# An expert layer in light positions: the down product one block later, the high half of the gated tile rounded by ScalarE

## The chip, the core and the metric

One core of a Trainium2 chip runs the whole program. The metric is the device time of one execution in microseconds; lower is better. TensorE multiplies, ScalarE and VectorE prepare its operands, and weights come from HBM through 16 DMA engines that SyncE's queue feeds.

## What is computed

The reference is an encoder trunk of two layers. Layer 0 ends in a dense SwiGLU, layer 1 in eight experts, of which each of the 256 tokens uses two:

```python
def swiglu(h, w1, w3, w2):
    return (jax.nn.silu(h @ w1) * (h @ w3)) @ w2

def moe_swiglu(h, w_router, w1, w3, w2):
    ...
    for e in range(N_EXPERTS):
        out = out + combine[..., e:e + 1] * swiglu(h, w1[e], w3[e], w2[e])
```

with model width 1024 and expert width 3584. The change touches the expert layer alone, which runs from about 700 us to the end.

## The kernel before

Every product is computed from operands that are split in two: `hi`, the value rounded to TensorE's format, and `lo`, the rest. A weight tile of 1 MB (128 x 2048 f32, an "item") is loaded into one of 7 `raw` buffers, ScalarE rounds it to `whi` (L1726), VectorE subtracts to get `wlo` (L2359), and TensorE uses both. `whi` and `wlo` have 3 slots (SPLIT), so the rounding of item n waits until TensorE has finished item n - 3. The load of item n + 7 is issued when `wlo` of item n is there (L1369). One list, `e_items`, fixes the order of items for all engines; each engine's program is written out by hand, and `e_room(phase, kind, n)` says how many items an engine may prepare before it has to do the named step.

Experts are visited in eight positions, `ROLES = "HLHLHLHH"`. A heavy position has room for 128 rows and uses hi and lo of the rows as separate operands. A light one has 64 rows and packs their hi and lo halves side by side into one 128-wide operand, so it needs two products where a heavy one needs three. Positions 1, 3 and 5 are light ("first", "second" and "third" light position below).

The expert width is cut into NM = 7 blocks (0 to 6). For each block there are six items: two halves of w1, two of w3, two of w2. In a position, TensorE does for block b = 1 to 6: `up` w1 b, `hidden_T` b - 1 (L1206: folds the packed halves and transposes them into the bank eT), `up` w3 b, `down` b - 1 (L1230). Then, in the tail: `up` w1 0 of the next position, `hidden_T` 6, `up` w3 0 of the next position, `down` 6. In blocks 1 to 6 and the tail one position takes 42 items; they are numbered 0 to 41 below, in the order in which they are used.

In a light position the gated tile of a block goes: ScalarE `silu_folded` (L1742), then on VectorE a multiplication into `gated_t` (L2385), the rounding of `gated_t` into the high half of `gated_m` (L2388), and the subtraction for its low half (L2390), which counts `g_lo` up; `down` waits for `g_lo`. All engines are strictly in order, so an instruction that waits holds back everything behind it on its engine.

Items before (`e_items`), in the lines that the change replaces:

```python
def mid_items(p):
    return [i for b in range(1, NM) for i in halves(p, ("w1", b), ("w3", b), ("w2", b - 1))]
...
    e_items += mid_items(p) + (head_items(p + 1) if p < LAST else []) + halves(p, ("w2", NM - 1))
```

Of the kernel before, what the change touches and what calls it, by code (L numbers as in the profile page):

```python
# [33 lines left out]
F32 = mybir.dt.float32  # L34
# [9 lines left out]
LIGHT = 64  # L44
# [202 lines left out]
def build(nc, x, mem, positions, g_mix, w_in, g_q, g_kv, w_uq, w_uk, w_uv, g_sg, w_s, b_s, g_mem,  # L247
# [31 lines left out]
    with ExitStack() as ctx:  # L279
# [285 lines left out]

        def halves(p, *blocks):
            return [(p, kind, b, half) for kind, b in blocks for half in range(2)]
# [4 lines left out]
        def mid_items(p):  # L572
            return [i for b in range(1, NM) for i in halves(p, ("w1", b), ("w3", b), ("w2", b - 1))]

        e_items = head_items(0)
        for p in range(NE):
            e_items += mid_items(p) + (head_items(p + 1) if p < LAST else []) + halves(p, ("w2", NM - 1))
# [120 lines left out]
        def _(pe):  # L698
# [467 lines left out]
            def is_light(phase):  # L1166
                return phase != "over" and light[phase]

# [84 lines left out]
            def blocks(phase, j=0):  # L1253

                for b_ in range(1, NM):
                    up(phase, "w1", b_, j)
                    if b_ == 1 and phase != "over" and phase and light[phase - 1]:
                        fold_result(phase - 1)
                    hidden_T(phase, b_ - 1, j)
                    if phase != "over" and phase < LAST and b_ == NM - 1:  # L1260

                        pe.wait_ge(slots_moved, 32 * phase + 16)
                        rows_T(phase + 1)
                    up(phase, "w3", b_, j)
                    if phase == LAST and b_ == NM - 1:
                        down(phase, b_ - 1, j, (0,))
                        hidden_T(phase, b_, j)
                        down(phase, b_ - 1, j, (1,))
                    else:
                        down(phase, b_ - 1, j)  # L1270
                    if phase == LAST and b_ == 2:
                        select_T(phase, j)
# [27 lines left out]
            for p in range(NE):  # L1300
                blocks(p)
                if p < LAST:
                    up(p + 1, "w1", 0, 0, lambda half: read(pe, (p + 1, "rows", half)))
                    hidden_T(p, NM - 1)
                    up(p + 1, "w3", 0)
                    down(p, NM - 1)
# [170 lines left out]
        def _(act):  # L1477
# [251 lines left out]
            def is_light(phase):  # L1729
                return phase != "over" and light[phase]  # L1730

# [11 lines left out]

            def copy_gate(p, b_):

                b = full(act, (p, "e3", b_))
                free(nc.scalar.activation(g32_m, b[:, :], ACT.Copy), (p, "e3", b_))

            def hidden_hi(phase, b_, j=0):

                b = full(act, (phase, "eT", b_), j)
                nc.scalar.activation(gated_m[0][:, b_ % 2, :], b[:, :], ACT.Copy).then_inc(g_hi, 1)
# [25 lines left out]
            def blocks(phase, j=0):  # L1778

                for b_ in range(1, NM):  # L1780
                    e_hi(e_room(phase, "e1", b_), j)
                    if is_light(phase):
                        e_hi(e_room(phase, "eT", b_ - 1), j)
                        silu_folded(phase, b_ - 1)
# [38 lines left out]
            for p in range(NE - 1):  # L1823
# [6 lines left out]
                if light[p]:  # L1830
                    e_hi(e_room(p, "eT", NM - 1))
                    silu_folded(p, NM - 1)
                e_silu(p + 1, 0)
                if not light[p]:
                    e_hi(e_room(p, "eT", NM - 1))
                    hidden_hi(p, NM - 1)
# [36 lines left out]
        def _(dve):  # L1873
# [489 lines left out]
            def is_light(phase):  # L2363
                return phase != "over" and light[phase]

# [7 lines left out]

            def hidden_lo(phase, b_, j=0):
# [5 lines left out]
                count = NM * (NE if phase == "over" else phase) + b_ + 1 + NM * j  # L2380
                if is_light(phase):
                    dve.wait_ge(silu_t_ready, light_block(phase, b_))
                    if light_block(phase, b_) > 1:
                        dve.wait_ge(g_lo, light_block(phase, b_) - 1)
                    free(V.tensor_tensor(gated_t, silu_t, b[:, BM * LIGHT:2 * BM * LIGHT], ALU.mult), (phase, "eT", b_))  # L2385
                    read(dve, (phase, "eT", b_))
                    part, by_chunk = by_slot(gated_m[0][:, b_ % 2, :]), gated_t.rearrange("p (c s) -> p c s", c=BM)
                    V.tensor_copy(part[:, :, 0:LIGHT], by_chunk).then_inc(g_hi, 1)  # L2388
                    dve.wait_ge(g_hi, count)
                    V.tensor_tensor(part[:, :, LIGHT:2 * LIGHT], by_chunk, part[:, :, 0:LIGHT].bitcast(F32),  # L2390
                                    ALU.subtract).then_inc(g_lo, 1)
                    return
                dve.wait_ge(g_hi, count)
# [36 lines left out]
            def blocks(phase, j=0):  # L2430

                for b_ in range(1, NM):
                    e_lo(e_room(phase, "e1", b_), j)
                    hidden_lo(phase, b_ - 1, j)
                    e_lo(e_room(phase, "e3", b_), j)
                    if phase != "over" and phase < LAST and b_ == NM - 1:
                        rows_lo(phase + 1)
                    hidden(phase, b_, j)
# [26 lines left out]
            for p in range(NE - 1):  # L2465
                blocks(p)
                e_lo(e_room(p + 1, "e1", 0))
                hidden_lo(p, NM - 1)
                e_lo(e_room(p + 1, "e3", 0))
                hidden(p + 1, 0)  # L2470
            dve.wait_ge(flag_ready, 1)
# [79 lines left out]
```

## Time and profile before

| | |
|---|---|
| median of 3 runs | 1626.28 us (1625.83 to 1626.38) |
| profiled execution | 1627.45 us |
| its span | 1625.6 us |
| TensorE busy, of the span | 97% |
| VectorE busy | 79% |
| ScalarE busy | 65% |
| mean granted TensorE clock | 0.994 |
| load, median from issue to landing (expert weights) | 8.0 us |

The span goes from the first to the last instruction; the 1.85 us between it and the profiled time lie around it. Busy shares are means over stages with different limits. A clock of 1.00 is 2.4 GHz, 0.50 is 1.2 GHz. In a timeline a line has start, length, engine, source line, operation, out<-in and count, and in brackets how long the engine sat idle before it and what ended that. A length includes the drain of the pipeline, so the next instruction of an engine can start before it is over; the pace of a row of instructions is read from starts. A line of a windows view has the stretch, its length, the busy time and count of TensorE (matmuls, then weight loads), VectorE, ScalarE and GpSimd, then TensorE's granted clock, the DMA share and GB/s.

### The profile page before, as it was taken

The numbers are of one execution on the slowest core, as the hardware profiler recorded it, in microseconds if no ns is written. First come the engines' busy times: TensorE is split into PE (matmuls) and PEld (weight loads), VectorE is DVE, ScalarE is ACT, GpSimd is POOL, SyncE is SP. The second block draws the span as 40 slices with busy tenths as digits, with TensorE's granted clock in tenths as the row PEclk, the third lists the DMA queues.
The fourth block names the chain that finished last, engine by engine and source line by source line (L and its number), as shares of the span: only waits on it lengthen the run. The fifth ranks groups of instructions, "written<-read, shape, count | busy, mean of one in ns | idle before, by whom it ended". The sixth has DMA issues, their size and how long they took to land.

```text
span 1625.6 us, 21020 instructions
## 1 busy us (share of the span) xinstructions
PE 1577.1 (97%) x8224; PEld 1336.8 (82%) x8224; DVE 1279.1 (79%) x1204; ACT 1057.5 (65%) x988; POOL 30.5 (2%) x69
## 2 busy tenths in 40 slices
PE   9999999999999999999999999999999999999997
PEld 8988888999989888778877778777788777788885
DVE  6676666555576756688899988899888999888997
ACT  6555445333355554557788877788777888777774
POOL 1000000000000000020000000000000000000100
PEclk9999999999999999999999999999999999999998
DMA  7654478977355535669999999999999999999992
GB/s 234 216 193 143 143 241 277 311 246 228 126 169 173 180 118 182 251 233 423 395 386 421 421 417 386 375 420 420 422 387 393 387 421 421 416 386 367 407 396 116
DMA packets 143112, 497.48 MB, mean 306 GB/s; under 512 B 8534, under 2 KB 64400, under 8 KB 100000
## 3 DMA queue, kind: packets, MB, share of 16 engines
q1 hardware_dynamic: 137008, 479.23, 77.8%
q0 software_dynamic: 2624, 8.45, 1.5%
q10 hardware_dynamic: 3376, 8.39, 1.3%
q8 instruction: 68, 1.11, 0.3%
q14 instruction: 36, 0.29, 0.1%
HBM read 476.64 MB, written 19.40 MB: 305 GB/s over the span
## 4 chain that ended last, share of the span: by engine, by line
PE 73%; DVE 18%; ACT 4%; issue 3%; DMA 1%; ACTq 0%; POOL 0%; SPq 0%; DVEq 0%; POOLq 0%
PE bank L730 22%; PE bank L1187 15%; PE bank L1230 13%; DVE wlo L2359 12%; PE bank L901 9%; PE bank L1191 8%; ACT whi L1726 2%; ACT whi L1493 1%; PE bank L720 1%; DVE wlo L1915 1%; PE bank L1015 1%; PE bank L1210 1%; PE bank L1206 1%; DMA hn<-in_mem 1%; ACT pbuf L1628 0%
## 5 line engine op out<-in xcount | busy, mean ns | idle before, releaser
L2359 DVE TENSOR_TENSOR wlo<-raw,whi 128x2048 fp32r<-128x2048 f32 x328 | 739.9, 2287 | 73.0 <-ACT whi L1726 72.4
L1726 ACT ACTIVATE whi<-raw 128x2048 fp32r<-128x2048 f32 x328 | 623.9, 1916 | 160.2 <-PE bank L1191 83.1
L1915 DVE TENSOR_TENSOR wlo<-raw,whi 128x2048 fp32r<-128x2048 f32 (+3 forms) x121 | 259.3, 2148 | 176.3 <-ACT whi L1493 175.9
L1493 ACT ACTIVATE whi<-raw 128x2048 fp32r<-128x2048 f32 (+3 forms) x121 | 217.7, 1801 | 145.8 <-PE bank L730 103.3
L1187 PE MATMUL bank<-whi,yT_hi 128*128 128x512 f32 x896 | 312.2, 396 | 0.0
L1191 PE MATMUL bank<-wlo,yT_hi 128*128 128x512 f32 x896 | 241.3, 391 | 2.9 <-DVE wlo L1915 2.8
L1187 PE MATMUL bank<-whi,yT_lo 128*128 128x512 f32 x560 | 216.7, 390 | 0.0
L1230 PE MATMUL bank<-whi,yT_hi 128*128 128x512 f32 x448 | 180.2, 402 | 25.7 <-DVE yT_hi L2390 16.4
L1191 PEld LDWEIGHTS bank<-wlo,yT_hi 128*128 128x128 f32 x896 | 168.3, 188 | 39.9 <-DVE wlo L1915 3.2
L1187 PEld LDWEIGHTS bank<-whi,yT_hi 128*128 128x128 f32 x896 | 167.0, 188 | 33.1
L1230 PE MATMUL bank<-wlo,yT_hi 128*128 128x512 f32 x448 | 175.9, 393 | 0.0
L1230 PEld LDWEIGHTS bank<-whi,yT_hi 128*128 128x128 f32 x448 | 84.5, 189 | 60.5 <-DVE yT_hi L2390 24.1
L730 PE MATMUL bank<-hT_hi,whi 128*128 128x256 f32 x464 | 131.4, 283 | 0.0
L730 PE MATMUL bank<-hT_hi,wlo 128*128 128x256 f32 x464 | 131.3, 283 | 0.0
L730 PE MATMUL bank<-hT_lo,whi 128*128 128x256 f32 x464 | 131.3, 283 | 0.0
L1187 PEld LDWEIGHTS bank<-whi,yT_lo 128*128 128x128 f32 x560 | 105.4, 188 | 21.3 <-DVE yT_lo L2298 0.2
L1230 PE MATMUL bank<-whi,yT_lo 128*128 128x512 f32 x280 | 109.0, 389 | 0.0
L1230 PEld LDWEIGHTS bank<-wlo,yT_hi 128*128 128x128 f32 x448 | 84.7, 189 | 16.8
L730 PEld LDWEIGHTS bank<-hT_lo,whi 128*128 128x128 f32 x464 | 89.0, 192 | 0.4
L730 PEld LDWEIGHTS bank<-hT_hi,whi 128*128 128x128 f32 x464 | 89.0, 192 | 0.4
L730 PEld LDWEIGHTS bank<-hT_hi,wlo 128*128 128x128 f32 x464 | 89.0, 192 | 0.0
L730 PE MATMUL bank<-whi,mT_hi 128*128 128x512 f32 (+1 forms) x204 | 79.6, 390 | 0.0
(323 smaller groups left out, 2062.8 us busy)
## 6 DMA issues: line engine op xcount, KB each, us to landing
raw<-in_moe_w SPq DMA_DIRECT2D x336, 1024.0 KB, 8.0
raw<-in_w_in SPq DMA_DIRECT2D x36, 1024.0 KB, 5.3
raw<-in_dense_w SPq DMA_DIRECT2D x30, 1024.0 KB, 6.4
raw<-in_w_br SPq DMA_DIRECT2D x12, 1024.0 KB, 5.0
rows_by_slot<-qxT SPq DMA_DIRECT2D x23, 512.0 KB, 7.0
raw<-in_w_out SPq DMA_DIRECT2D x8, 1024.0 KB, 5.0
raw<-in_w_mkv SPq DMA_DIRECT2D x6, 1024.0 KB, 8.2
cqkv<-rows_by_slot ACTq DMA_DIRECT2D x7, 512.0 KB, 8.5
```

The source lines that it names most:

```text
L720: ins = nc.tensor.matmul(bank, lhs(k), rhs(k), start=(k == 0), stop=(k == n - 1))
L730: ins = nc.tensor.matmul(bank, lhs(a, k), rhs(b, k), start=(start and k == chunks[0] and a + b == 0), stop=(stop and k == chunks[-1] and a ...
L901: ins = nc.tensor.matmul(bank, src(a, x0), w[b_][:, w0, :], start=(start and q + i == 0), stop=(stop and last))
L1015: ins = nc.tensor.matmul(b[:, t * SEQ:(t + 1) * SEQ], qT[0:QK, h, tok(t)], kT[0:QK, h, :], start=True, stop=True)
L1187: nc.tensor.matmul(b[:, :], hselT[a][:, half, tok(k)], w[:, k, :], start=(half + k + a == 0), stop=False)
L1191: ins = nc.tensor.matmul(b[:, :], hselT[0][:, half, tok(k)], w[:, k, :], start=False, stop=(half == 1 and k == 3))
L1206: ins = nc.tensor.matmul(b[:, a:a + LIGHT], src[:, tok(c)], fold[:, 0:LIGHT], start=True, stop=True)
L1230: ins = nc.tensor.matmul(banks[4 + n][:, :], gated_m[a][:, b_ % 2, tok(2 * half + c)], w[p][:, c, n * HALF:(n + 1) * HALF], start=(b_ + ha ...
L1493: nc.scalar.activation(whi[:, m % SPLIT, 0:floats(n)], raw[:, pieces[n][1], 0:floats(n)], ACT.Copy).then_inc(hi_ready, 1)
L1726: nc.scalar.activation(whi[:, (E0 + n) % SPLIT, :], raw[:, n % RAW, :], ACT.Copy).then_inc(hi_ready, 1)
L1915: V.tensor_tensor(wlo[:, m % SPLIT, 0:size], raw[:, pieces[n][1], 0:size], whi[:, m % SPLIT, 0:size].bitcast(F32), ALU.subtract).then_inc( ...
L2359: V.tensor_tensor(wlo[:, s, :], raw[:, n % RAW, :], whi[:, s, :].bitcast(F32), ALU.subtract).then_inc(lo_ready, 1)
```

## The change

In light positions (`light[p]`) the down product of a block runs one block later: w2 b - 2 in block b, nothing in block 1, and w2 5 and w2 6 one after the other in the tail. `hidden_lo` of a light block is divided: `gated` (VectorE) writes `gated_t`, `hidden_hi` on ScalarE rounds it into the high half, and `gated_lo` (VectorE) subtracts one block later. In the tail of a light position the three parts for block 6 follow one another. Heavy positions keep their order. `is_light` moves to one place.

```diff
             return w[0, :, b, half, :, :][e, :, :].unsqueeze(1)
 
 
+        def is_light(phase):
+            return phase != "over" and light[phase]
+
         def halves(p, *blocks):
             return [(p, kind, b, half) for kind, b in blocks for half in range(2)]
 
...
             return halves(p, ("w1", 0), ("w3", 0))
 
         def mid_items(p):
-            return [i for b in range(1, NM) for i in halves(p, ("w1", b), ("w3", b), ("w2", b - 1))]
+            lag = 2 if is_light(p) else 1
+            return [i for b in range(1, NM)
+                    for i in halves(p, ("w1", b), ("w3", b), *([("w2", b - lag)] if b >= lag else []))]
+
+        def tail_items(p):
+            return halves(p, *([("w2", NM - 2)] if is_light(p) else []), ("w2", NM - 1))
 
         e_items = head_items(0)
         for p in range(NE):
-            e_items += mid_items(p) + (head_items(p + 1) if p < LAST else []) + halves(p, ("w2", NM - 1))
+            e_items += mid_items(p) + (head_items(p + 1) if p < LAST else []) + tail_items(p)
         N_E = len(e_items)
         PER_E = N_E // NE
         HEAD = len(head_items(0))
...
                         down(phase, b_ - 1, j, (0,))
                         hidden_T(phase, b_, j)
                         down(phase, b_ - 1, j, (1,))
-                    else:
+                    elif not is_light(phase):
                         down(phase, b_ - 1, j)
+                    elif b_ > 1:
+                        down(phase, b_ - 2)
                     if phase == LAST and b_ == 2:
                         select_T(phase, j)
 
...
                     up(p + 1, "w1", 0, 0, lambda half: read(pe, (p + 1, "rows", half)))
                     hidden_T(p, NM - 1)
                     up(p + 1, "w3", 0)
+                    if light[p]:
+                        down(p, NM - 2)
                     down(p, NM - 1)
             combine(LAST)
             marks["over"] = [count, 0]
...
                 b = full(act, (p, "eT", b_))
                 nc.scalar.activation(silu_t, b[:, 0:BM * LIGHT], ACT.Silu).then_inc(silu_t_ready, 1)
 
+            def hidden_hi(phase, b_, j=0):
+
+                if is_light(phase):
+                    read(act, (phase, "eT", b_))
+                    nc.scalar.activation(by_slot(gated_m[0][:, b_ % 2, :])[:, :, 0:LIGHT],
+                                         gated_t.rearrange("p (c s) -> p c s", c=BM), ACT.Copy).then_inc(g_hi, 1)
+                    return
+                b = full(act, (phase, "eT", b_), j)
+                nc.scalar.activation(gated_m[0][:, b_ % 2, :], b[:, :], ACT.Copy).then_inc(g_hi, 1)
+
             def copy_gate(p, b_):
 
                 b = full(act, (p, "e3", b_))
                 free(nc.scalar.activation(g32_m, b[:, :], ACT.Copy), (p, "e3", b_))
-
-            def hidden_hi(phase, b_, j=0):
-
-                b = full(act, (phase, "eT", b_), j)
-                nc.scalar.activation(gated_m[0][:, b_ % 2, :], b[:, :], ACT.Copy).then_inc(g_hi, 1)
 
             def rows_hi_part(phase, j=0):
 
...
                 for b_ in range(1, NM):
                     e_hi(e_room(phase, "e1", b_), j)
                     if is_light(phase):
-                        e_hi(e_room(phase, "eT", b_ - 1), j)
+                        if b_ > 1:
+                            hidden_hi(phase, b_ - 2)
+                        e_hi(e_room(phase, "eT", b_ - 1))
                         silu_folded(phase, b_ - 1)
                     e_silu(phase, b_, j)
                     if b_ == 1 and phase != "over" and phase and light[phase - 1]:
...
                 rows_hi_part(p + 1)
                 e_hi(e_room(p + 1, "e1", 0))
                 if light[p]:
+                    hidden_hi(p, NM - 2)
                     e_hi(e_room(p, "eT", NM - 1))
                     silu_folded(p, NM - 1)
                 e_silu(p + 1, 0)
-                if not light[p]:
-                    e_hi(e_room(p, "eT", NM - 1))
-                    hidden_hi(p, NM - 1)
+                e_hi(e_room(p + 1, "e3", 0) if light[p] else e_room(p, "eT", NM - 1))
+                hidden_hi(p, NM - 1)
                 if light[p + 1]:
                     e_hi(e_room(p + 1, "e3", 0))
                     copy_gate(p + 1, 0)
...
                 read(dve, (phase, "e1", b_), j)
                 free(V.tensor_tensor(g32_m, silu_m, b[:, :], ALU.mult), (phase, "e3", b_))
 
+            def gated(p, b_):
+
+                b = full(dve, (p, "eT", b_))
+                dve.wait_ge(silu_t_ready, light_block(p, b_))
+                if light_block(p, b_) > 1:
+                    dve.wait_ge(g_lo, light_block(p, b_) - 1)
+                free(V.tensor_tensor(gated_t, silu_t, b[:, BM * LIGHT:2 * BM * LIGHT], ALU.mult), (p, "eT", b_))
+
+            def gated_lo(p, b_):
+
+                dve.wait_ge(g_hi, NM * p + b_ + 1)
+                part = by_slot(gated_m[0][:, b_ % 2, :])
+                V.tensor_tensor(part[:, :, LIGHT:2 * LIGHT], gated_t.rearrange("p (c s) -> p c s", c=BM),
+                                part[:, :, 0:LIGHT].bitcast(F32), ALU.subtract).then_inc(g_lo, 1)
+
             def hidden_lo(phase, b_, j=0):
 
                 end = N_E + PER_E if phase == "over" else N_E
                 last = phase in (LAST, "over") and b_ == NM - 1
                 e_lo(min(e_room(phase, "eT", b_), end - 1 if last else end), j)
                 b = full(dve, (phase, "eT", b_), j)
-                count = NM * (NE if phase == "over" else phase) + b_ + 1 + NM * j
-                if is_light(phase):
-                    dve.wait_ge(silu_t_ready, light_block(phase, b_))
-                    if light_block(phase, b_) > 1:
-                        dve.wait_ge(g_lo, light_block(phase, b_) - 1)
-                    free(V.tensor_tensor(gated_t, silu_t, b[:, BM * LIGHT:2 * BM * LIGHT], ALU.mult), (phase, "eT", b_))
-                    read(dve, (phase, "eT", b_))
-                    part, by_chunk = by_slot(gated_m[0][:, b_ % 2, :]), gated_t.rearrange("p (c s) -> p c s", c=BM)
-                    V.tensor_copy(part[:, :, 0:LIGHT], by_chunk).then_inc(g_hi, 1)
-                    dve.wait_ge(g_hi, count)
-                    V.tensor_tensor(part[:, :, LIGHT:2 * LIGHT], by_chunk, part[:, :, 0:LIGHT].bitcast(F32),
-                                    ALU.subtract).then_inc(g_lo, 1)
-                    return
-                dve.wait_ge(g_hi, count)
+                dve.wait_ge(g_hi, NM * (NE if phase == "over" else phase) + b_ + 1 + NM * j)
                 part = [v[:, b_ % 2, :] for v in gated_m]
                 free(V.tensor_tensor(part[1], b[:, :], part[0].bitcast(F32), ALU.subtract), (phase, "eT", b_))
 
...
 
                 for b_ in range(1, NM):
                     e_lo(e_room(phase, "e1", b_), j)
-                    hidden_lo(phase, b_ - 1, j)
+                    if not is_light(phase):
+                        hidden_lo(phase, b_ - 1, j)
+                    elif b_ > 1:
+                        gated_lo(phase, b_ - 2)
                     e_lo(e_room(phase, "e3", b_), j)
                     if phase != "over" and phase < LAST and b_ == NM - 1:
                         rows_lo(phase + 1)
+                    if is_light(phase):
+                        gated(phase, b_ - 1)
                     hidden(phase, b_, j)
                     if phase == LAST and b_ == 1:
                         last_choice()
...
             for p in range(NE - 1):
                 blocks(p)
                 e_lo(e_room(p + 1, "e1", 0))
-                hidden_lo(p, NM - 1)
+                if light[p]:
+                    gated_lo(p, NM - 2)
+                else:
+                    hidden_lo(p, NM - 1)
                 e_lo(e_room(p + 1, "e3", 0))
+                if light[p]:
+                    gated(p, NM - 1)
                 hidden(p + 1, 0)
+                if light[p]:
+                    gated_lo(p, NM - 1)
             dve.wait_ge(flag_ready, 1)
             overflow = dve.value_load(more[0:1, 0:1], min_val=0, max_val=1)
             blocks(LAST)
```

## Rows read from the trace of the kernel before

**Rows 1.** Profile page: its first line.
```profile
span 1625.6 us, 21020 instructions
```

**Rows 2.** Windows: blocks of the first light position, then a heavy one.
```profile
834.00:918.00 84.00, 77.16 (x379) 61.93 (x378) 82.49 (x55) 72.73 (x56) 0.00 (x0) 1.00 1.01 421
...
942.00:1030.00 88.00, 87.87 (x401) 72.19 (x400) 75.01 (x42) 65.68 (x44) 0.00 (x0) 1.00 1.00 394
```

**Rows 3.** Timeline of VectorE, first light position, blocks 4 to 6.
```profile
884.49 0.41 DVE L2385 TENSOR_TENSOR cT<-cT,bank 128x256 f32<-128x256 f32 x1
884.93 0.29 DVE L2388 CAST yT_hi<-cT 128x256 fp32r<-128x256 f32 x1
885.26 0.43 DVE L2390 TENSOR_TENSOR yT_hi<-cT,yT_hi 128x256 fp32r<-128x256 f32 x1
885.60 13.29 DVE L2359 TENSOR_TENSOR wlo<-raw,whi 128x2048 fp32r<-128x2048 f32 x6
898.81 0.41 DVE L2385 TENSOR_TENSOR cT<-cT,bank 128x256 f32<-128x256 f32 x1
...
914.56 2.29 DVE L2359 TENSOR_TENSOR wlo<-raw,whi 128x2048 fp32r<-128x2048 f32 x1 [0.22 <-ACT whi L1726]
```

**Rows 4.** Timeline of VectorE: item 2 of each of the three light positions.
```profile
834.88 6.70 DVE L2359 TENSOR_TENSOR wlo<-raw,whi 128x2048 fp32r<-128x2048 f32 x3 [1.49 <-ACT whi L1726]
...
1057.78 6.69 DVE L2359 TENSOR_TENSOR wlo<-raw,whi 128x2048 fp32r<-128x2048 f32 x3 [1.49 <-ACT whi L1726]
...
1281.82 6.69 DVE L2359 TENSOR_TENSOR wlo<-raw,whi 128x2048 fp32r<-128x2048 f32 x3 [1.49 <-ACT whi L1726]
```

**Rows 5.** Timeline of TensorE, first light position, blocks 4 and 5.
```profile
888.03 0.47 PE L1230 MATMUL bank<-whi,yT_hi 128*128 128x512 f32 x1 [0.18 <-DVE wlo L2359]
...
893.58 1.89 PE L1206 MATMUL bank<-cT,sgv 128*128 128x64 f32 x16
895.28 1.18 PE L1187 MATMUL bank<-whi,yT_hi 128*128 128x512 f32 x4
...
897.21 1.08 PE L1187 MATMUL bank<-whi,yT_hi 128*128 128x512 f32 x4
...
900.07 0.50 PE L1230 MATMUL bank<-whi,yT_hi 128*128 128x512 f32 x1 [0.87 <-DVE yT_hi L2390]
```

**Rows 6.** Timeline of ScalarE, first light position, and block 6 of the third.
```profile
897.47 1.92 ACT L1726 ACTIVATE whi<-raw 128x2048 fp32r<-128x2048 f32 x1 [0.96 <-PE bank L1191]
...
910.36 0.36 ACT L1742 ACTIVATE cT<-bank 128x256 f32<-128x256 f32 x1
...
912.61 1.92 ACT L1726 ACTIVATE whi<-raw 128x2048 fp32r<-128x2048 f32 x1 [1.41 <-PE bank L1191]
...
1353.75 1.92 ACT L1726 ACTIVATE whi<-raw 128x2048 fp32r<-128x2048 f32 x1 [0.34 <-DMA raw<-in_moe_w]
```

**Rows 7.** Loads by tile: items 29 and 33; each took 11.5 us.
```profile
L1372 SPq DMA_DIRECT2D raw<-in_moe_w x1: 333/333/333, 884.6 to 884.6; - x1
...
L1372 SPq DMA_DIRECT2D raw<-in_moe_w x1: 333/333/333, 894.5 to 894.5; - x1
...
DMA to landing us min/median/max: 11.5/11.5/11.5
```

**Rows 8.** Timeline of TensorE, tail of the first light position.
```profile
928.93 0.39 PE L1187 MATMUL bank<-whi,yT_hi 128*128 128x512 f32 x1
...
931.65 0.39 PE L1230 MATMUL bank<-whi,yT_hi 128*128 128x512 f32 x1
...
935.50 0.40 PE L1187 MATMUL bank<-whi,yT_hi 128*128 128x512 f32 x1
```

**Rows 9.** TensorE after a long wait: timeline, and one window's clock.
```profile
712.34 2.08 PE L1191 MATMUL bank<-wlo,yT_hi 128*128 128x512 f32 x4 [2.80 <-DVE wlo L1915]
...
1065.65 0.50 PE L1230 MATMUL bank<-whi,yT_hi 128*128 128x512 f32 x1 [1.89 <-DVE yT_hi L2390]
...
1068.00:1070.00 2.00, 2.00 (x7) 1.57 (x6) 2.00 (x1) 1.44 (x1) 0.00 (x0) 0.50 0.99 418
```

More of the change, by code:

```diff
@@ L1164, in e_part @@
                 return tile[:, (E0 + n) % SPLIT, :].rearrange("p (k c) -> p k c", k=k)
-            def is_light(phase):
-                return phase != "over" and light[phase]
             def up(phase, kind, b_, j=0, rows=None):
@@ L1727, in e_hi @@
                 n_done = max(n_done, end)
-            def is_light(phase):
-                return phase != "over" and light[phase]
             def e_silu(phase, b_, j=0):
@@ L2361, in e_lo @@
                 n_done = max(n_done, end)
-            def is_light(phase):
-                return phase != "over" and light[phase]
             def hidden(phase, b_, j=0):
```

## The prediction

> **What bounds the kernel.** I read the first line of the page, then windows by stage, then timelines of single blocks, then the landing of single loads. The profiled execution took 1627.45 us for a span of 1625.6 [rows 1]. The windows show two limits at once in the light positions: VectorE is busy for 82.5 of 84 us and TensorE for 77.2, while the DMA engines are full at 421 GB/s; in the heavy position TensorE is busy all the time, and the DMA has some air (394 GB/s) [rows 2]. So the end moves by what a light position takes, and a heavy one passes every shift on.
>
> The timeline of VectorE shows a light block: from the multiplication at 884.49 to the next at 898.81 there are 14.32 us without a gap. Three small instructions take 1.11 (0.44 + 0.33 + 0.34, by starts), six subtractions 13.21, so 2.20 each [rows 3]. TensorE waits 0.87 for that chain before `down`, and 0.18 for the next item [rows 5]. All three light positions begin alike: item 2 is subtracted at 834.88, 1057.78 and 1281.82 [rows 4]. I work out the first one and shift it.
>
> **The hidden limit.** Items 29 and 33 were asked for at 884.6 and 894.5, and both landed 11.5 later, at 896.1 and 906.0: four loads in 9.9, so 2.48 us each [rows 7]. A light block needs six items in 14.32, one each 2.39 [rows 3]. The position lives on what was loaded ahead, and in the third one the stock runs out: item 33 waits for its load, to 1353.75 [rows 6], which is 906.81 in the first position's time (less 446.94, rows of item 2 [rows 4]). Asking earlier lands nothing earlier, as the engines are full.
>
> The Trainium skill (DMA: Bandwidth & Descriptors, Where 436 GB/s comes from) gives 435 GB/s as the ceiling of the fabric and about 358 for a core's HBM side. The trace's 421 lies just under the first and above the second, so for one core alone the first is nearer. By 435 a load would take 2.41 us, which is an estimate from the page, and the cap below would nearly go.
>
> **Part 1: the cast leaves VectorE.** The rounding (0.33 by starts) goes, and the multiplication no longer waits for its successor (0.44 becomes about 0.33, as 0.41 long with the overlap that its neighbours show). A block then costs VectorE 13.21 + 0.33 + 0.34 = 13.88 instead of 14.32. ScalarE gets the rounding: the trace has no ScalarE instruction of that form; nearest are `silu_folded` at 0.36 for 128 x 256 [rows 6] and, as the other bound, VectorE's own 0.29 [rows 3]. I take 0.36. ScalarE is busy for 73 of 84 us there [rows 2], so inside a block it is hidden; without that cover it would cost 0.36 for each of 21 blocks, 7.6 us.
>
> **Part 2: down one block later.** TensorE no longer waits for the chain. Item 33 is now the last of block 6 (w2 of block 4); w2 of block 5, two items, is pushed into the tail. Paced by VectorE alone, its subtraction would start at 834.88 + 31 x 2.20 + 5 x 0.33 + 5 x 0.34 = 906.4; I add 0.1 for small waits, 906.5. But its load lands at 906.0, and ScalarE start to VectorE start is 1.95 (912.61 to 914.56 [rows 3, 6]): 908.0 at the earliest. The cap eats 1.5 us; in the third position, with 906.8, it gives 908.8 and eats 2.3.
>
> **From there to the tail**, in TensorE's time. VectorE start to `down` start is 2.43 (885.60 to 888.03 [rows 3, 5]), so item 33 runs from 910.4. A light half takes 1.93 (931.65 to 935.50 is two [rows 8]), a heavy half 2.72 (928.93 to 931.65 [rows 8]), `hidden_T` 1.70 (893.58 to 895.28 [rows 5]). Item 33 1.93, items 34 and 35 5.44, `hidden_T` 1.70, item 36 about 2.8: it ends at 922.3. Before, the same item (first half of w3 0) ended at 928.93 [rows 8]. Of these 6.6 us, 3.9 are only the two halves of `down` 5 that are still owed. The real gain so far is 2.7.
>
> **Part 3: the tail gives it back.** Call the end of item 36 zero. TensorE: item 37 to 2.72, `down` 5 (38, 39) to 4.65 and 6.58. Next is `down` 6, item 40. ScalarE must round item 39 first, from 0.26 (as 897.21 to 897.47 [rows 5, 6]). VectorE subtracts it at 0.26 + 1.95 = 2.21, and only behind it, at 4.41, comes `gated` 6, done at 4.82. ScalarE's next instruction is `hidden_hi` 6, which waits for exactly that; behind it stands the rounding of item 40, which could have begun at 2.98, when item 37 was out. It begins at about 5.2 (0.36 after 4.85). Then VectorE at 7.16, TensorE at 9.59. It had been done at 6.58: it stalls for 3.0 us. Item 41 follows one subtraction later, at 11.79, and ends at 13.7. Of the stall 0.8 (2.98 + 1.95 + 2.43 = 7.36) would be there without that wait too, since four short halves in a row outrun the three slots; before, two heavy halves stood there. The queues of SyncE (load n + 7 behind `wlo` n) are delayed by 2 to 3 us for the loads behind item 40, which took over 10 us to land and stay hidden. GpSimd's queue is not touched.
>
> So `down` 6 ends at 922.3 + 13.7 = 936.0 where it ended at 935.5: 0.5 later in the first and the second light position, and 1.3 later in the third (0.8 more by the landing). Sum 2.3 us slower. Behind it TensorE is the limit, so it stays.
>
> **Part 4: TensorE's clock.** After the wait of 2.80 at 712.34 four matmuls took 2.08 us, against 1.08 for four at 897.21 [rows 5, 9]. After the wait of 1.89 at 1065.65 the granted clock was 0.50 (1.2 GHz) in 1068 to 1070 [rows 9], while the same wait in the first and third position left it at 1.00. The change removes these three waits, and makes three of 3.0 us. I take it that the clock falls behind each. The price is between 1.0 (four matmuls at half clock) and 2.0 (eight); I take 1.6, less the 0.3 that TensorE would wait anyway between items 40 and 41: 1.3 each, 3.9 in all.
>
> The Trainium skill (TensorE: Matmul & The Clock Gate, Why this matters for your kernels) warns of idle gaps between bursts of matmuls of about the length that I forecast, and calls shorter ones safe. The 1.89 row contradicts that. By the page the new stalls stand just at its edge; if they are on its safe side, case (a) below results.
>
> **The sum.** The profiled execution is 1.17 over the median, about what one such dip costs, so I take the timed runs to be without it: the sum against the profiled execution is 1627.45 - 1.2 + 2.3 + 3.9 = 1632.5 (the dip goes with its wait), and against the median 1626.28 + 2.3 + 3.9 = 1632.5.
>
> **Rivals.**
> (a) The clock holds behind the new stalls. For it: three waits of 1.6 to 1.9 left it alone; against: both rows of rows 9. 1626.28 + 2.3 = 1628.6, which counts as the same.
> (b) Faster: the loads don't cap. If loads asked for earlier also land earlier, the position is paced by VectorE up to item 33 (906.5), and each position gains 1.0 net of the tail; it decides once load 33 lands before 904.5. 1626.28 - 3.0 = 1623.3, if the clock holds too. Against it: the even 2.48 between landings.
> (c) The clock stays low for a whole heavy item as well, 2.6 instead of 1.3 each: 1636.4. For it: nothing shown, the dip had ended after some 3 us.
>
> **How the numbers follow.** Forecast 0.50, (a) 0.26, (b) 0.12, (c) 0.12. 0.2% is 3.25 us, about what a measurement can tell. Slower is the forecast and (c), 0.62; same is (a), 0.26; faster is (b), 0.12. The range goes from 1623.0, just under (b), to 1635.0, which leaves room for a price of 2.0 instead of 1.6 per fall and for 1.2 of error in the tails; (c) lies outside.
>
> **What would show it.** After: L2388 gone, and 21 ScalarE instructions of 128 x 256 more at about 0.36; light blocks of about 13.9 on VectorE until ScalarE waits for loads in blocks 5 and 6; TensorE without its waits for the chain inside blocks; in each tail a wait of about 3.0 before the first matmul of `down` 6, and a granted clock of 0.50 behind it. I am wrong if that wait is under 2, or the clock stays at 1.00, or load 33 lands much before 906.

## The result: 2.1 us slower, and the profile after

| | before | after |
|---|---|---|
| median | 1626.38 us (1624.89 to 1628.46, 13 runs) | 1628.52 us (1626.97 to 1632.25, 13 runs) |
| profiled execution | 1627.45 | 1627.16 |
| its span | 1625.6 | 1625.2 |

The ratio is 1.0017, with a 95% interval of 1.001 to 1.0024, which is 2.8 us; the medians differ by 2.1. The changed kernel is slower, but by less than the 0.2% (3.25 us) that I set as the bound, so by my own rule this is "same", the verdict of rival (a). The forecast was 1632.5, 4.0 over the result; rival (a), in which the clock holds, gave 1628.6.

The page after, its parts on span and busy time and the row of the new rounding (instructions, then busy us and mean ns, then idle time ahead of it). VectorE has 21 instructions less and ScalarE 21 more, each 402 ns where I took 360; of the idle 8.1 us each tail has 2.7.

```profile
span 1625.2 us, 21020 instructions
...
PE 1581.2 (97%) x8224; PEld 1336.2 (82%) x8224; DVE 1272.8 (78%) x1183; ACT 1064.4 (65%) x1009; POOL 30.6 (2%) x69
...
L1754 ACT ACTIVATE yT_hi<-cT 128x256 fp32r<-128x256 f32 x21 | 8.5, 402 | 8.1 <-DVE cT L2390 8.1
```

Timeline of VectorE after, blocks 2 to 4 of the first light position and its tail (L2390 is `gated`, L2396 `gated_lo`, L2372 the subtraction to `wlo`, L2382 `hidden`). It answers to [rows 3]: a block is 13.97 and 13.94 us long (851.43, 865.40, 879.34) where it was 14.32; 13.88 was forecast.

```profile
851.43 0.41 DVE L2390 TENSOR_TENSOR cT<-cT,bank 128x256 f32<-128x256 f32 x1
...
865.40 0.41 DVE L2390 TENSOR_TENSOR cT<-cT,bank 128x256 f32<-128x256 f32 x1
...
879.34 0.41 DVE L2390 TENSOR_TENSOR cT<-cT,bank 128x256 f32<-128x256 f32 x1
...
922.90 2.29 DVE L2372 TENSOR_TENSOR wlo<-raw,whi 128x2048 fp32r<-128x2048 f32 x1 [1.47 <-ACT whi L1735]
925.11 0.41 DVE L2390 TENSOR_TENSOR cT<-cT,bank 128x256 f32<-128x256 f32 x1
925.44 0.68 DVE L2382 TENSOR_TENSOR sgv<-sgv,bank 128x512 f32<-128x512 f32 x1
926.04 0.42 DVE L2396 TENSOR_TENSOR yT_hi<-cT,yT_hi 128x256 fp32r<-128x256 f32 x1
927.81 8.90 DVE L2372 TENSOR_TENSOR wlo<-raw,whi 128x2048 fp32r<-128x2048 f32 x4 [1.35 <-ACT whi L1735]
```

Timeline of ScalarE after: block 4, where it begins to wait for loads, and the tail. ScalarE stands idle for 2.69 us ahead of `hidden_hi` 6 (L1754), until `gated` 6 is done, and the rounding of item 40 starts right behind it, at 925.88.

```profile
881.86 1.92 ACT L1735 ACTIVATE whi<-raw 128x2048 fp32r<-128x2048 f32 x1 [0.45 <-DMA raw<-in_moe_w]
...
920.95 1.92 ACT L1735 ACTIVATE whi<-raw 128x2048 fp32r<-128x2048 f32 x1 [1.47 <-PE bank L1196]
925.56 0.42 ACT L1754 ACTIVATE yT_hi<-cT 128x256 fp32r<-128x256 f32 x1 [2.69 <-DVE cT L2390]
925.88 5.50 ACT L1735 ACTIVATE whi<-raw 128x2048 fp32r<-128x2048 f32 x3
```

Timeline of TensorE after, tail of the first light position, answering to [rows 8]: `down` 6 starts after a wait of 2.82 and the next item starts at 934.37. The position began 1.74 earlier than before (item 2 at 833.14, against 834.88 in [rows 4]), so that is 936.11 in the old time, against 935.50.

```profile
930.25 0.47 PE L1235 MATMUL bank<-whi,yT_hi 128*128 128x512 f32 x1 [2.82 <-DVE wlo L2372]
...
934.37 0.40 PE L1192 MATMUL bank<-whi,yT_hi 128*128 128x512 f32 x1
```

Windows after: the stretch of the first light position that [rows 2] show, then two microseconds behind the wait in each tail. The clock fell in the second and the third.

```profile
834.00:918.00 84.00, 80.47 (x398) 64.16 (x398) 83.08 (x49) 75.82 (x62) 0.00 (x0) 1.00 1.01 421
930.00:932.00 2.00, 1.75 (x8) 1.42 (x8) 2.00 (x2) 1.39 (x1) 0.00 (x0) 1.00 1.02 422
...
1154.00:1156.00 2.00, 2.00 (x6) 1.50 (x5) 2.00 (x2) 0.83 (x1) 0.00 (x0) 0.54 1.01 422
...
1380.00:1382.00 2.00, 2.00 (x6) 1.59 (x5) 2.00 (x2) 0.40 (x1) 0.00 (x0) 0.50 1.02 422
```

**Where the time went.** Item 2 starts at 833.14, 1056.65 and 1281.35 after, so the first position took 223.51 (222.90 before [rows 4]): 0.61 more at full clock. The second took 224.70, which is 223.51 and 1.19 for the fall. From the third item 2 to the first `hT_lo`, which closes the experts, it is 330.31 against 328.72, so 0.35 more once 1.24 for the fall is taken off. Between the start of `down` 6 and the next item there are 4.12 us in the first tail, 5.35 and 5.36 in the others: that is the 1.24.

The rest stands at the very end. The timelines of VectorE there, before:

```profile
1611.90 0.69 DVE L2452 TENSOR_TENSOR hT_lo<-bank,hT_hi 128x512 fp32r<-128x512 f32 x1 [0.67 <-ACT hT_hi L1818]
...
1616.85 1.23 DVE L2507 TENSOR_TENSOR hn<-x_sb,mkT 128x1024 f32<-128x1024 f32 x1 [1.63 <-issue]
...
1620.43 1.41 DVE L2511 SCALAR_TENSOR_TENSOR hn<-x_sb,rin,mkT 128x512 f32<-128x512 f32 x2
```

and after:

```profile
1613.02 0.69 DVE L2469 TENSOR_TENSOR hT_lo<-bank,hT_hi 128x512 fp32r<-128x512 f32 x1 [0.67 <-ACT hT_hi L1831]
...
1616.26 1.21 DVE L2531 TENSOR_TENSOR hn<-x_sb,mkT 128x1024 f32<-128x1024 f32 x1
...
1620.03 1.41 DVE L2535 SCALAR_TENSOR_TENSOR hn<-x_sb,rin,mkT 128x512 f32<-128x512 f32 x2
```

From the last `hT_lo` to `hn` it is 4.95 before and 3.24 after, though the source of this stretch is the same. Between the two lies the branch past a skipped `If`. Of these 1.7 us, 0.2 are given back at once: from `hn` to the last instruction it is 3.58 before and 3.77 after. So 1.5 us of gain at the end were in no step of mine.

The two profiled spans differ by 0.4 the other way (1625.6 and 1625.2), and that is chance: the profiled execution after was already 1.74 ahead at the first item 2, where the change has done nothing yet, and before's clock had also fallen between 12 and 14 us, where after's stayed at 1.00. With 0.61, 0.66 (224.70 against 224.04, with a fall in both) and 1.59 for the three positions and -1.52 for the end, -1.74 gives the -0.4.

```profile
12.00:14.00 2.00, 2.00 (x12) 2.00 (x11) 2.00 (x5) 1.87 (x3) 0.00 (x0) 0.54 1.14 332
```

### The profile page after: what moved, and what is told of

Read it like the earlier page. It is cut to its first block, busy times and chain, and to the rows that moved or that the text cites. A ratio compares the mean times of both kernels' runs of the same rounds, so it can differ in the third digit from the quotient of the medians.

```text
span 1625.2 us, 21020 instructions
## 1 busy us (share of the span) xinstructions
PE 1581.2 (97%) x8224; PEld 1336.2 (82%) x8224; DVE 1272.8 (78%) x1183; ACT 1064.4 (65%) x1009; POOL 30.6 (2%) x69
## 4 chain that ended last, share of the span: by engine, by line
PE 71%; DVE 16%; ACT 5%; issue 4%; DMA 3%; ACTq 0%; POOL 0%; DVEq 0%; POOLq 0%
PE bank L738 21%; PE bank L1192 14%; PE bank L1235 13%; DVE wlo L2372 11%; PE bank L909 9%; PE bank L1196 7%; DMA raw<-in_moe_w 2%; ACT whi L1735 2%; ACT whi L1502 1%; PE bank L728 1%; DVE wlo L1928 1%; PE bank L1023 1%; PE bank L1215 1%; DMA hn<-in_mem 1%; ACT pbuf L1637 0%
## 5 line engine op out<-in xcount | busy, mean ns | idle before, releaser
L2372 DVE TENSOR_TENSOR wlo<-raw,whi 128x2048 fp32r<-128x2048 f32 x328 | 742.9, 2287 | 84.1 <-ACT whi L1735 83.4
```

What stands on the lines that cost most here:

```text
L2372: V.tensor_tensor(wlo[:, s, :], raw[:, n % RAW, :], whi[:, s, :].bitcast(F32), ALU.subtract).then_inc(lo_ready, 1)
```

## The experiments

All ratios are against the kernel before on the same chips.

| kernel | median us | ratio, 95% interval |
|---|---|---|
| e1 gated early in the tail | 1619.31 | 0.9956 (0.9941 to 0.997) |
| e2 20 matmuls in the wait | 1628.61 | 1.0011 (1.0002 to 1.002) |
| e3 after, half loads | 1625.57 | 0.9997 (0.9988 to 1.0006) |
| e4 before, half loads | 1626.03 | 0.9996 (0.9987 to 1.0005) |
| e5 12 matmuls in the wait | 1625.54 | 0.9994 (0.9985 to 1.0003) |
| e6 e1 and item 40 earlier | 1620.9 | 0.9963 (0.995 to 0.9977) |
| e7 lag alone | 1625.45 | 0.999 (0.9981 to 0.9999) |
| e8 rounding on ScalarE alone | 1631.72 | 1.0031 (1.0019 to 1.0044) |
| e9 e1 and items 40, 41 earlier | 1618.55 | 0.9957 (0.9944 to 0.9971) |
| e10 before, 24 met waits | 1626.11 | 1.0003 (0.9994 to 1.0012) |
| e11 after, 24 met waits | 1628.48 | 1.0014 (1.0004 to 1.0023) |
| e12 after, 54 met waits | 1632.14 (1 run) | |

### The order in the tail (e1)

```diff
-                e_lo(e_room(p + 1, "e3", 0))
                 if light[p]:
+                    e_lo(e_room(p, "eT", NM - 1))
                     gated(p, NM - 1)
+                e_lo(e_room(p + 1, "e3", 0))
                 hidden(p + 1, 0)
```

> The changed kernel, but in the tail of a light position VectorE multiplies block 6 (gated) before the subtraction of item 39, not behind it. Theory (ScalarE's rounding of block 6 waits for that multiplication and holds back the rounding of item 40): ScalarE's wait of 2.7 us ahead of that rounding goes, TensorE's wait before the down product of block 6 falls from 3.0 to about 1.2, each light position ends 1.8 us earlier than in the changed kernel, and the clock no longer falls behind it. Time 3 to 6 us under the kernel before. Rival (the loads set the end of a light position, the tail only shows it): the wait of ScalarE turns into a wait for loads or for TensorE, and the time stays about 2 us over the kernel before.

Timelines of ScalarE, VectorE and TensorE in the tail of e1, first light position:

```profile
919.64 1.92 ACT L1735 ACTIVATE whi<-raw 128x2048 fp32r<-128x2048 f32 x1 [1.62 <-PE bank L1196]
921.46 0.40 ACT L1754 ACTIVATE yT_hi<-cT 128x256 fp32r<-128x256 f32 x1
922.36 3.73 ACT L1735 ACTIVATE whi<-raw 128x2048 fp32r<-128x2048 f32 x2 [0.50 <-PE bank L1196]
```

```profile
920.08 0.41 DVE L2390 TENSOR_TENSOR cT<-cT,bank 128x256 f32<-128x256 f32 x1
921.59 2.29 DVE L2372 TENSOR_TENSOR wlo<-raw,whi 128x2048 fp32r<-128x2048 f32 x1 [1.09 <-ACT whi L1735]
```

```profile
927.16 0.47 PE L1235 MATMUL bank<-whi,yT_hi 128*128 128x512 f32 x1 [1.05 <-DVE wlo L2372]
```

`gated` 6 runs in VectorE's idle time ahead of item 39, so `hidden_hi` 6 no longer waits, and the rounding of item 40 waits only for its slot. The wait of TensorE falls from 2.82 to 1.05, and no clock falls behind it. The kernel is 9.2 us under after and 6.8 under before, more than the 3 to 6 expected: most of the stall in the tail was the order of two instructions. In the profile the three positions are 5.0 shorter than after's without its falls (1.8, 1.4 and 1.9); the falls that are gone are worth 3.0 to 3.7 more, as e5 shows below.

### How often and how dearly the clock falls (e2, e5)

20 (e2) or 12 (e5) matmuls of the identity, 128 x 128, into a free bank, between `down` 5 and `down` 6:

```diff
                         down(p, NM - 2)
+                        spare = claim((LAST, "selT", 0))
+                        for _ in range(12):
+                            nc.tensor.matmul(spare[:, 0:P], ident[:, :], ident[:, :], start=True, stop=True)
                     down(p, NM - 1)
```

> The changed kernel with 20 extra 128x128 matmuls into an unused bank between the down products of blocks 5 and 6, where TensorE stands still for 3.0 us. Theory (a fall of the clock behind the stall costs 1.24 us each time it happens, and makes the runs of the changed kernel scatter from 1627.0 to 1632.3): the real down product of block 6 starts at the same time after item 36 (9.6 us), the granted clock stays 1.00 there, the runs lie within about 1.5 us of each other, and the median is 1 to 2 us under the changed kernel's, so within 1 us of the kernel before. Rival (the clock doesn't matter; the scatter comes from elsewhere): same median as the changed kernel (+2) and the same scatter.

> The changed kernel with 12 extra matmuls (24 passes of 0.11 us, 2.6 us) in the 3.0 us stall of the tail; 20 of them took 4.4 us, longer than the stall, and delayed the real ones by about 1 us. Theory (a fall of the clock behind the stall costs 1.24 us and happens some two times of three in each run): the clock stays 1.00 in the tails, the real down product of block 6 starts as in the changed kernel, and the median falls by 2 to 3 us below the changed kernel's 1628.5, to about 1626. Rival (the clock costs next to nothing on average): about 1628.5 as without the filling.

In e2 the 20 took 4.4 us, which is 1.4 longer than the stall, and cost what the clock gave back. In e5 the 12 took 2.84, as long as the stall. Windows of e5 in the three tails:

```profile
930.00:932.00 2.00, 1.85 (x11) 1.43 (x10) 2.00 (x2) 1.63 (x1) 0.00 (x0) 1.00 1.01 422
...
1154.00:1156.00 2.00, 1.94 (x8) 1.26 (x8) 2.00 (x2) 1.00 (x1) 0.00 (x0) 1.00 0.99 414
1380.00:1382.00 2.00, 2.00 (x10) 1.65 (x9) 2.00 (x2) 2.00 (x3) 0.00 (x0) 1.00 1.02 426
```

The clock holds in all three, and the median is 3.0 under after's; by the two ratios to before it is 3.7. Two falls of 1.24 in three tails are 2.5, three are 3.7: the timed runs have two or three each. In the profiles of the four kernels with the full stall (after, e3, e11, e12) the clock fell in 8 of 12 tails; with waits up to 1.73 (e1, e6, e7, e9) in none of 12.

One of the eight, the second tail of e12, stayed down for twice as long: from `down` 6 to the next item it is 6.60 us, against 4.12 at full clock, so that fall cost 2.5. This is what rival (c) had supposed for every tail. Windows of e12 there:

```profile
1156.00:1158.00 2.00, 2.00 (x6) 1.52 (x6) 2.00 (x2) 0.68 (x1) 0.00 (x0) 0.50 1.00 418
...
1160.00:1162.00 2.00, 2.00 (x7) 1.57 (x6) 0.66 (x1) 1.80 (x2) 0.00 (x0) 0.57 1.03 422
```

With it the four profiles come to 9 times 1.24 in four executions, 2.8 each, which fits the 3.0. The wait near 710 us, at the start of the experts [rows 9], is of the same length, 2.76 to 2.80, and in all 14 profiles; behind it the clock fell in ten and held in four (e1, e4, e8, e9). It makes every kernel here scatter, before too. In e4 it held, and the same four matmuls take 1.20 where they took 2.08 in before:

```profile
710.41 1.20 PE L1191 MATMUL bank<-wlo,yT_hi 128*128 128x512 f32 x4 [2.79 <-DVE wlo L1919]
```

### Do the loads cap the light positions? (e3, e4)

In light positions each load brings half of its columns; the rest of the buffer is left as it was, so the products are of other numbers.

```diff
+                if phase != "over" and light[phase]:
+                    cut = src.shape[2] // 2
+                    dst, src = dst[:, :, 0:cut], src[:, :, 0:cut]
                 sp.dma_start(dst, src).then_inc(raw_in[slot], 16)
```

> The changed kernel, but items of light positions load only half of their columns (the other half of the buffer keeps old weights, so the output is not the reference's; all other work is the same). Theory (the DMA engines cap the light blocks at item 33, 1.5 us over VectorE's own pace): no waits of ScalarE for loads; item 33 is subtracted about 71.6 us after item 2 instead of 73.1; the wait in the tail stays 3.0; time 3 to 5 us under the changed kernel. Rival (the loads are hidden, blocks are paced by VectorE or by a loop over all three engines): 73.1 stays, time as the changed kernel.

> The kernel before with the same half loads in light positions (output not the reference's). Theory: its light blocks are paced by VectorE (14.3 us each) and use the loads just as they land, so the time changes by less than 1 us. Rival (the loads bound the kernel before too): 3 us or more faster.

Timeline of VectorE in e3, item 33, then that of ScalarE. No wait for a load is left, and item 33 still waits 0.82, for ScalarE, which had stood behind TensorE:

```profile
906.14 2.29 DVE L2376 TENSOR_TENSOR wlo<-raw,whi 128x2048 fp32r<-128x2048 f32 x1 [0.82 <-ACT whi L1739]
```

```profile
889.40 1.92 ACT L1739 ACTIVATE whi<-raw 128x2048 fp32r<-128x2048 f32 x1 [0.82 <-PE bank L1196]
...
904.18 1.92 ACT L1739 ACTIVATE whi<-raw 128x2048 fp32r<-128x2048 f32 x1 [1.60 <-PE bank L1196]
```

Item 33 comes 72.73 us after item 2 (833.41), where it is 73.13 in after (833.14 to 906.27). Free loads are worth 0.4 us per position here, not the 1.5 of my step. The pace of VectorE alone, 71.6, is not reached even then. ScalarE's wait for a slot of TensorE is 1.60 in block 6 and 0.82 one block earlier, and what TensorE does more in block 6 is the row transposes for the next position, 0.8 us (901.20 to 902.00). That they are the cause is read from this match; no run takes them out. Before is not bound by loads either (e4, no change), as both theories had it. Of the 3.0 us between e3's and after's medians three times 0.4 is 1.2; the rest I can't place, since falls of the clock differ from run to run by as much. Nor do the loads always keep up: in e11's first position item 33 comes 74.33 after item 2, 1.2 later than in after, behind waits for loads in block 4.

### Each half of the change alone (e7, e8)

e7 has the new order and leaves the rounding on VectorE, inside `gated_lo`. e8 has the order of before with the rounding on ScalarE, behind the last item of the block:

```diff
                         e_hi(e_room(phase, "e3", b_))
+                        hidden_hi(phase, b_ - 1)
                         copy_gate(phase, b_)
...
-                    V.tensor_copy(part[:, :, 0:LIGHT], by_chunk).then_inc(g_hi, 1)
                     dve.wait_ge(g_hi, count)
```

> The down product one block later as in the change, but VectorE still rounds the high half itself, right before the low half. Theory: light blocks take VectorE 14.2 to 14.3 us, so item 33 comes about 1 us later than in the changed kernel (73.1 us after item 2), but in the tail ScalarE has nothing to wait for: the stall before the down product of block 6 is about 1.9 instead of 3.0. Together about 0.5 us per position better than the changed kernel, and fewer falls of the clock: 1625 to 1627. Rival (what costs is the pair of down products in the tail, whoever rounds): the stall stays near 3.0 and the time is over 1628.5.

> The kernel before, with its order of down products, but the high half rounded by ScalarE behind the rounding of the block's last item. Theory: VectorE's three small instructions become two with a hand-over in between (0.41 + 0.03 + 0.40 + 0.03), so it stands still as long as it worked before: light blocks of 14.3 to 14.5 us, the wait of TensorE 0.9 to 1.0, time 0 to 3 us over the kernel before. Rival (the rounding was the cost): 0.33 us off each of 21 blocks, some 5 us faster.

e7: blocks of 14.21, and in the first tail TensorE waits 1.73, not 2.82, as ScalarE has no `hidden_hi` to hold the rounding of item 40 back; the clock holds in all three. Timeline of TensorE in its first tail:

```profile
930.02 0.47 PE L1235 MATMUL bank<-whi,yT_hi 128*128 128x512 f32 x1 [1.73 <-DVE wlo L2369]
```

e8 is the slowest of the timed ones, 5.2 over before. Timeline of VectorE, blocks 4 and 5:

```profile
882.19 0.41 DVE L2393 TENSOR_TENSOR cT<-cT,bank 128x256 f32<-128x256 f32 x1
883.17 0.43 DVE L2397 TENSOR_TENSOR yT_hi<-cT,yT_hi 128x256 fp32r<-128x256 f32 x1 [0.56 <-ACT yT_hi L1753]
...
896.72 0.41 DVE L2393 TENSOR_TENSOR cT<-cT,bank 128x256 f32<-128x256 f32 x1
```

The round trip takes 0.98 from `gated` to the subtraction where it was 0.77 with the cast between [rows 3]: VectorE stands 0.56 in place of its own 0.33, the block grows to 14.53. The price is higher still at the end of a light position, where VectorE waits 1.39 and 2.12 for the rounding of the last two blocks; the position takes 225.32, 2.4 more than before. The two halves are not a sum: ScalarE's rounding pays only with the lag around it, and the lag alone loses nothing.

### What is left in the tail (e6, e9)

e1, with `gated_lo` 6 and the subtraction of item 40 (e6: + 1) or of items 40 and 41 (e9: + 2) ahead of `hidden`:

```diff
                 e_lo(e_room(p + 1, "e3", 0))
+                if light[p]:
+                    gated_lo(p, NM - 1)
+                    e_lo(e_room(p + 1, "e3", 0) + 2)
                 hidden(p + 1, 0)
-                if light[p]:
-                    gated_lo(p, NM - 1)
```

> As e1_gated_early, and VectorE also does the low half of block 6 and the subtraction of item 40 ahead of the product for the next position's w3. Theory (what is left of the stall is the three-slot loop alone, 0.8 us, and VectorE's order): the wait before the down product of block 6 goes from 1.1 to about 0.8, each position ends another 0.4 us earlier, time about 1 us under e1's 1619.3. Rival (the rest of the stall is not VectorE's order): as e1.

> The kernel with the early gated multiplication in the tail, and on VectorE now gated_lo 6 and the subtractions of both last items (40 and 41) ahead of the next position's multiplication. My theory (what is left in the tail is the order of VectorE's queue, item 41 deciding after the kernel with item 40 alone in front): the 0.71 us wait before item 41 goes, the multiplication that is now last is hidden, and the kernel gains up to 0.4 us per light position on the one with the early gated multiplication alone (1619.31), so about 1618. Rival (the three slots and the loads decide, not the order): 1619 to 1621, with the waits only moved, since the next position's multiplication then comes too late for its own consumers.

Timeline of TensorE in e6, items 40 and 41, and of e9, item 40:

```profile
929.15 0.47 PE L1235 MATMUL bank<-whi,yT_hi 128*128 128x512 f32 x1 [0.64 <-DVE wlo L2372]
931.95 0.47 PE L1235 MATMUL bank<-whi,yT_hi 128*128 128x512 f32 x1 [0.71 <-DVE wlo L2372]
```

```profile
926.91 0.47 PE L1235 MATMUL bank<-whi,yT_hi 128*128 128x512 f32 x1 [0.63 <-DVE wlo L2372]
```

e6 missed: its wait came back ahead of item 41, behind the multiplication that now stood between. e9 has no such second wait. Its positions take 221.62 and 221.63 (item 2 at 831.68, 1053.30, 1274.93) against 221.74 and 222.13 in e1. It has the lowest median, 0.8 under e1, but the ratios to before are all but equal (0.9957 and 0.9956): that it beats e1 is not shown, that both beat before and after is.

### The 1.6 us at the end (e10 to e12)

24 or 54 more waits on a semaphore that has its value, ahead of the branch; nothing else differs.

```diff
-            dve.wait_ge(flag_ready, 1)
+            for _ in range(25):
+                dve.wait_ge(flag_ready, 1)
             overflow = dve.value_load(more[0:1, 0:1], min_val=0, max_val=1)
```

> The kernel before, with 24 more waits that are already met on VectorE just ahead of the last branch, so that all of VectorE's later instructions lie elsewhere in memory; nothing else differs. Theory (the 1.6 us for which VectorE stands in 'issue' ahead of its third-last instruction depend on where its instruction stream lies): that idle time changes, and goes to about 0 if the stream's position decides, and the time falls by up to 1.6 less about 1 for the added waits. Rival (it belongs to the rounding on VectorE, or to chance): still 1.6 us of issue there, 4.9 to 5.2 us from the last hT_lo to the end row.

> The changed kernel with the same 24 met waits. Theory (position of the instruction stream): the end, 3.24 us from the last hT_lo to the next row now, may become 4.9 to 5.2, with an idle time of about 1.6 put down to issue. Rival (it belongs to what the change does to the instructions): 3.24 as now.

> The changed kernel with 54 met waits where the last one had 24. The last pair kept its ends as they were (issue wait with the order of before, none with the changed one), and the profile counts 12 instructions more for 24 waits, so 54 waits are 27 instructions. Theory (the place of VectorE's instruction stream decides, and 12 instructions were too small a shift): the kernel with the lag alone is the changed kernel with about 21 more VectorE instructions and has the wait; so with 27 more the idle time of about 1.6 us put down to issue appears ahead of the third-last row, and the last hT_lo to that row takes 4.9 to 5.2 us in place of 3.24. Rival (it is not the place of the stream): 3.24 as in the changed kernel.

The pages count 21032 instructions with 24 waits, 12 more. With them nothing changed at the end: 4.96 and a wait of 1.64 in e10, 3.24 in e11. With 54 waits (27 instructions) the wait appears in the changed kernel. Timeline of VectorE in e12:

```profile
1616.57 0.69 DVE L2469 TENSOR_TENSOR hT_lo<-bank,hT_hi 128x512 fp32r<-128x512 f32 x1 [0.67 <-ACT hT_hi L1831]
...
1621.56 1.22 DVE L2532 TENSOR_TENSOR hn<-x_sb,mkT 128x1024 f32<-128x1024 f32 x1 [1.66 <-issue]
```

The wait stands in six of the 14 profiles (before, e4, e7, e8, e10, e12) and in none of the others. What VectorE does is not the cause: e8 has no rounding on VectorE and has the wait, and e12 has it with nothing added but waits that are met. What is left is how its instructions lie; e12 is one execution, so this rests on one row. Its time, 1632.14, is no measure of this: the double fall in its second tail is in it.

## Why the prediction was nearly right, step by step

The forecast was 4.0 us too high. That the result lands on the number of rival (a) is luck: its condition, that the clock holds, is false, and gains that no step had stand against the falls.

- **Direction and mechanism: right.** The tail gives back what the blocks gain. Item 36 ended at 922.43 in the old time (922.3 forecast); `down` 6 waited 2.82, 2.83 and 2.83 (3.0 forecast), with the releasers that Part 3 names. e1 shows that the named instruction was the cause of 1.77 of each.
- **Part 1: right.** Blocks of 13.95 for 13.88, the rounding 0.40 for 0.36 and hidden. e8 shows the price when it is not: more than the 0.33 that leaves.
- **Part 2: time right, reason wrong.** Item 33 came at 908.01 in the old time, 908.0 forecast. But "the cap eats 1.5 us" is mis-sized: e3 gives 0.4. The rest of the delay stands behind TensorE's slots, most likely its row transposes of block 6, which my pace of 31 subtractions left out. Rival (b) could therefore not have gained what I priced.
- **"1.3 later in the third position": mis-sized.** It was 0.35. The stock of loads ran no shorter there than in the others: item 33 comes 73.21 after item 2, against 73.13 and 73.09.
- **"Three falls of the clock at 1.3": the price right, the count too high.** A fall costs 1.24, but in the profile the clock fell in two of three tails, and e5 puts all falls of a run at 3.0 (medians) to 3.7 us (ratios), not 3.9. The Trainium skill (TensorE: Matmul & The Clock Gate, Why this matters for your kernels) warns of idle gaps of about the length of these tails. The traces show chance on both sides of that advice: the clock held behind 4 of 12 tails of 2.8 us, and fell behind 3 of the 9 waits of 1.89 to 1.90 in before, e4 and e10, while e8's three of 2.08 to 2.09 left it at 1.00.
- **Missing.** The changed kernel also loses a dip of its own: "the dip goes with its wait" stood in the sum against the profiled execution, and was taken as absent from the timed runs. The profiles of before, e4 and e10 each have one in some light position, so the timed runs have about one too. And the 1.5 us at the end were in no step.
- **The sum again, from rows:** 0.61 + 0.61 + 0.35 for the tails, 3.0 for the falls, less 1.1 for before's own dip, less 1.5 at the end: 2.0, where the medians differ by 2.1. With 3.7 for the falls it is 2.7, where the ratio gives 2.8. It is not an independent forecast, since the falls are taken from e5's time.

## What to carry to other kernels

When an operation is moved to a less busy engine, look at what is queued behind it there: in the tail a 0.4 us rounding held the next weight's rounding for 2.7 us, and moving its producer up by one place was worth 9 us. Compute the pace of a loop over all engines whose slots it passes, with everything one block does and the others don't, before a delay is put down to loads. Under 2 us, look at the profile's end first: here a stretch of code that wasn't touched became 1.7 us shorter, and longer again with 54 met waits ahead of it.

## What was not expected of the hardware

- Behind the skipped `If` VectorE stands 1.6 to 1.9 us in "issue", or not at all: with the changed kernel not, nor with 12 instructions more, but with 27 more. That it is the loading of code is likely and not shown: the queue of instruction packets of the profile has 36 packets in before, e7, e8 and e12, which wait, and 35 in after and e1, which don't; but e11 has 36 and doesn't. At what boundary it happens stays open.
- The same wait of TensorE, 2.82 to 2.83 us, had the clock fall behind it in two tails of one execution and not in the third, and once, in e12, for twice as long.
- A matmul of 128 x 128 f32 by the identity stands in the trace as two entries and takes 0.22 us in all (20 in 4.4), so that filling a gap needs half as many as one would guess from the 0.11 of one entry.
